# Reordering the borders and the second layer of a two-block transformer kernel on one Trainium2 core

## The reference

```
# block one, layers 1 and 2
u = rmsnorm(h, norm_pre[i]); y = mixer(u); h = h + rmsnorm(y, norm_post[i])
# dilated_mixer (layer 1): q,k,v,gate = split(u @ w_in); q,k = rope(q),rope(k)
#   windowed softmax attention of each group, groups merged by softmax of their log denominators
y = o * silu(gate) @ w_out
# diff_mixer (layer 2), per head and block of 128 queries
s = einsum(q, k) * scale                      # two score matrices, c = 0, 1
s = where(kpos <= qpos, s, -inf); p = softmax(s)
a = p[:, 0] - lam * p[:, 1]
o = rmsnorm(einsum(a, v), subln) * (1.0 - lambda_init)
y = o * silu(gate) @ w_out
# block two, twice
y = (sigmoid(gate_a) * (sparse_attention @ p_attn)
     + sigmoid(gate_b) * (gated_linear_attention @ p_gla)) @ w_out + b_out
x = layer_norm(DN_ALPHA * x + y)
u = conv3(x @ w_up) + conv_b; a, b = split(u)
x = layer_norm(DN_ALPHA * x + (gelu(a) * b) @ w_down)
```

## Time and profile before

| | |
|---|---|
| runs | 2937.83, 2944.55, 2944.97 us (median 2944.55) |
| profiled execution | 2947.25 us, span 2945.9 us, mean granted TensorE clock 0.982 |
| PE busy | 2787.2 us (95%) |
| DVE, ACT, POOL busy | 1256.2, 1092.0, 1068.4 us |
| HBM traffic | 90 GB/s over the span |

### The profile page before, as it was taken

The page is one execution under the profiler, slowest core; times in us unless marked ns, Lnnn a source line. Parts: engine busy times, 40 slices in busy tenths (PEclk is TensorE's granted clock), DMA queues, the critical chain, the costliest instruction groups (busy, mean ns, idle before and its releaser), DMA issues.

```text
span 2945.9 us, 39012 instructions
## 1 busy us (share of the span) xinstructions
PE 2787.2 (95%) x15161; PEld 2288.2 (78%) x15161; DVE 1256.2 (43%) x2777; ACT 1092.0 (37%) x2037; POOL 1068.4 (36%) x854
## 2 busy tenths in 40 slices
PE   6999999989989899999999999999999999999997
PEld 5887878788767777766688888887776668888887
DVE  3344444444455437433425424255642343542425
ACT  3444344443444433453323424233435332242422
POOL 3333334222332233332343454435342235444442
PEclk9999999999999899999999999999999999999999
DMA  4322223231111222222344232223222224423222
GB/s 143 87 87 87 82 77 94 80 125 57 60 57 56 79 92 86 72 79 82 97 150 137 72 115 77 95 86 120 72 73 78 86 86 158 134 75 100 98 89 72
DMA packets 247547, 269.06 MB, mean 91 GB/s; under 512 B 11582, under 2 KB 208930, under 8 KB 246596
## 3 DMA queue, kind: packets, MB, share of 16 engines
q1 hardware_dynamic: 247364, 266.56, 27.9%
HBM read 247.59 MB, written 18.94 MB: 90 GB/s over the span
## 4 chain that ended last, share of the span: by engine, by line
PE 80%; DVE 8%; ACT 4%; issue 3%; POOL 2%; DMA 2%; SPq 0%; DVEq 0%; ACTq 0%; POOLq 0%
PE banks L1457 43%; PE banks L1454 24%; DVE AR L2110 2%; POOL WS L2676 2%; PE banks L1475 2%; PE banks L1576 2%; PE banks L1525 1%; PE banks L1683 1%; ACT WS L1783 1%; PE banks L1559 1%; DVE SM L2110 1%; PE banks L1731 1%; PE banks L1499 1%; PE banks L1544 1%; PE banks L1647 1%
## 5 line engine op out<-in xcount | busy, mean ns | idle before, releaser
L2676 POOL TENSOR_TENSOR WS<-WR,WS 128x512 fp32r<-128x512 f32 (+1 forms) x772 | 974.1, 1294 | 1561.5 <-ACT WS L1783 1561.5
L1457 PE MATMUL banks<-WS,UT 128*128 128x512 f32 (+1 forms) x5712 | 1217.4, 363 | 26.3 <-issue 7.2
L1457 PEld LDWEIGHTS banks<-WS,UT 128*128 128x128 f32 x5712 | 920.5, 192 | 203.5 <-issue 63.4
L1454 PE MATMUL banks<-UT,WS 128*128 128x512 f32 (+1 forms) x2928 | 691.1, 395 | 0.6 <-issue 0.6
L1454 PEld LDWEIGHTS banks<-UT,WS 128*128 128x128 f32 (+1 forms) x2928 | 547.8, 189 | 128.6 <-issue 14.1
L1783 ACT ACTIVATE WS<-WR 128x1024 fp32r<-128x1024 f32 (+2 forms) x408 | 395.1, 1021 | 121.8 <-PE banks L1457 63.1
L1457 PE MATMUL banks<-WS,AT 128*128 128x256 f32 (+1 forms) x1776 | 305.6, 332 | 21.3 <-DVE AT L2110 21.3
L1457 PEld LDWEIGHTS banks<-WS,AT 128*128 128x128 f32 x1776 | 266.2, 191 | 57.6 <-DVE AT L2110 16.8
L2639 DVE SCALAR_TENSOR_TENSOR AR<-banks,AR 128x511 f32<-128x511 f32 x88 | 66.0, 750 | 227.5 <-ACT AR L2090 227.5
L2110 DVE TENSOR_TENSOR AR<-AR 128x256 f32<-128x256 f32 (+2 forms) x169 | 147.7, 893 | 18.8 <-ACT AR L2022 7.4
L2691 POOL TENSOR_TENSOR SM<-SM 128x1 f32<-128x1 f32 (+2 forms) x44 | 46.9, 1067 | 282.0 <-DVE SM L2615 121.1
(11 more groups left out here) (205 smaller groups left out, 2665.8 us busy)
## 6 DMA issues: line engine op xcount, KB each, us to landing
WR<-in_w_in SPq DMA_DIRECT2D x56, 1024.0 KB, 5.1
WR<-in_w_up SPq DMA_DIRECT2D x44, 1024.0 KB, 5.1
WR<-in_dil_w_in SPq DMA_DIRECT2D x128, 256.0 KB, 4.0
WR<-in_w_down SPq DMA_DIRECT2D x16, 1024.0 KB, 5.0
WR<-in_dil_w_in SPq DMA_DIRECT2D x8, 1024.0 KB, 5.1
WR<-in_diff_w_in SPq DMA_DIRECT2D x16, 512.0 KB, 4.3
WR<-in_diff_w_in SPq DMA_DIRECT2D x8, 1024.0 KB, 5.5
spill<-AR SPq DMA_DIRECT2D x32, 256.0 KB, 3.3
```

The source lines that it names most:

```text
L1454: mm = pe.matmul(B[bank][0:c, :], w[x][:, kk, g * P:g * P + c], act[:, y, kk, :], start=start, stop=stop)
L1457: mm = pe.matmul(B[bank][:, off:off + n], act[:, x, before_k + kk, g * P:g * P + P], w[y][:, kk, :], start=start, stop=stop)
L2676: ge.tensor_tensor(slot(i, 1)[:, s], raw(i)[:, s], slot(i, 0)[:, s].bitcast(F32), ALU.subtract).then_inc(lo_p.sem, 1)
```

## The change

It has these parts:

- **Layer 2 a step deeper.** An empty stage stands between scores and mix, and MF serves as a third score buffer. `norm2` is one step of two operations, three ticks later; the factor subln (a DMA of 128 x 1 in place of 128 x 128) is applied when the chunks of layer 2 are split.
- **No negation.** The mask step of layers 1 and 2 scales by -0.125 and takes the minimum, so the small operation behind it goes.
- **Low parts in single steps.** POOL's four quarters of a tile become four steps `lo`, one of them issued per tick, all before the tile is used.
- **Borders by parts.** Chunks 0 to 3 stand beside the gate projections; chunks 4 to 7 stand between parts of the output projection: (tile, from part, to part) = (0,0,4), (1,0,4), (0,4,6), (1,4,6), (2,0,6), (0,6,8), (1,6,8), (2,6,8). The third tile comes in at the fifth place. In `wide` with fresh input the first two token blocks go through both half tiles before the last blocks are needed.
- **The last up tile by token halves.** b10 goes as (tokens 0 to 255, both feature blocks), then (256 to 511), with its convolution, product and split by halves; d20, d21 and d22 follow with all six parts for the first block.
- **Weight tiles in halves.** Each load is two transfers with a semaphore each; half v of tile i + 2 may start when half v of tile i has been split.

```diff
+    def by_pool(self, i):
+        return i > 0 and not (self.grouped[i] and i % 2)
     def split(self):
-        self.step("split", self.splits)
+        i = self.splits
+        self.step("split", i)
+        if self.by_pool(i):
+            self.lows += [(i, v) for v in range(4)]
         self.splits += 1
+    def lower(self, i):
+        while self.lows and self.lows[0][0] <= i:
+            self.step("lo", *self.lows.pop(0))
...
     def tick(self, n=1):
...
+        for _ in range(n):
+            if self.lows:
+                self.step("lo", *self.lows.pop(0))
...
+        walk = [(half, b) for half in range(2) for b in range(first, NB)]
+        if fresh and name != "l1a0":
+            walk = [(half, b) for half in range(2) for b in (first, first + 1)]
+            walk += [(half, b) for b in range(first + 2, NB) for half in range(2)]
...
+    def opening(turns):
+        parts = [(0, 0, 4), (1, 0, 4), (0, 4, 6), (1, 4, 6), (2, 0, 6), (0, 6, 8), (1, 6, 8), (2, 6, 8)]
+        for n, what in enumerate(turns):
+            parts.insert(2 * n, what)
+        return parts
...
+                    if half and j < 2:
+                        self.soon(4, lambda: self.step("chunk", name, 2 * j))
+                        self.soon(6, lambda: self.step("chunk", name, 2 * j + 1))
...
-            yield from self.pipelined(len(units), lambda n: units[n][0] in projected, [scores, mix, turn, out_of])
+            yield from self.pipelined(len(units), lambda n: units[n][0] in projected,
+                                      [scores, lambda n: (), mix, turn, out_of])
...
+            if (kind, j) == ("b", 10):
+                i = self.open(f"f{l}b10")
+                for half in range(2):
+                    for c in range(2):
+                        self.bank[i, c, half] = 2 - 2 * half + c
+                        self.step("last", l, i, c, half)
+                        self.step("conv_last", l, i, c, half)
+                        self.tick(2)
...
-        self.by_blocks([f"f{l}d2{c}" for c in range(4)], finish, lambda: None)
+        self.by_blocks([f"f{l}d2{c}" for c in range(4)], finish, [(j, 0, 6) for j in range(3)], order=(2, 3, 0, 1))
...
-                                                    CT[:, C_CM + 512 - w:C_CM + 512], 1.0, GONE, ALU.add, ALU.max,
-                                                    SM[:, MX + 2 * e + c:MX + 2 * e + c + 1])
+                    for c in range(2):
+                        x = ve.tensor_tensor_reduce(S2(n, c, w), B[4 + c][:, 0:w], CT[:, C_CM + 512 - w:C_CM + 512],
+                                                    -0.125, -GONE, ALU.add, ALU.min, small2(n, "max", c))
                     x.then_inc(maxed.sem, 1)
-                    ve.wait_ge(maxed.sem, maxed.at["2", n])
-                    ve.tensor_scalar(SM[:, NBI + 2 * e:NBI + 2 * e + 2], SM[:, MX + 2 * e:MX + 2 * e + 2], -0.125, None,
-                                     ALU.mult).then_inc(negated.sem, 1)
...
-            def load_tile(i):
+            def load_half(i, v):
                 _, k, n, pieces = tiles[i]
                 dst = raw(i).rearrange("p (k n) -> p k n", k=k)
+                part = slice(v * k // 2, (v + 1) * k // 2)
                 for c, src in pieces:
-                    sy.dma_start(dst[:, :, c:c + src.shape[2]], src).then_inc(tile_in[i % 2].sem, 16)
+                    sy.dma_start(dst[:, part, c:c + src.shape[2]], src[:, part, :]).then_inc(tile_in[2 * (i % 2) + v].sem, 16)
```

More of the change, by code:

```diff
@@ L366, in feature_major, with by_blocks @@
             yield 2
-    def by_blocks(self, names, finish, late):
+    def by_blocks(self, names, finish, opening, order=(0, 1, 2, 3)):
         i0 = self.opened
@@ L374, in by_blocks @@
             split = b == 0
-            banks = ((0, 1, 2, 3), (4, 5), (0, 1), (2, 3))[b]
-            early = [0] * 4
-            if split:
-                for j in range(2):
-                    ws.append(self.open(names[j]))
+            banks = (order, (4, 5), (0, 1), (2, 3))[b]
+            for what in opening if split else ():
+                if isinstance(what[0], str):
+                    self.step(*what)
+                else:
+                    j, k0, k1 = what
+                    if len(ws) == j:
+                        ws.append(self.open(names[j]))
                     self.bank[ws[j], b] = (banks[j], 0)
-                    early[j] = self.tiles[ws[j]][1] - 2
-                    self.step("mm", ws[j], b, 0, early[j])
-                late()
+                    self.step("mm", ws[j], b, k0, k1)
+                    self.tick()
             for j in range(4):
@@ L525, in layer1 @@
         self.fill(self.opened + 2)
-        self.by_blocks([f"l1o{j}" for j in range(4)], self.residual("l1o"), lambda: self.last_quarter("l1g", late))
+        self.lower(self.opened + 1)
+        for x in late:
+            self.step("times", *x)
+        self.by_blocks([f"l1o{j}" for j in range(4)], self.residual("l1o"),
+                       self.opening([("chunk", "l1g", c) for c in range(4, 8)]))
     def layer2(self):
@@ L576, in layer2 @@
         self.beside(self.gates("l2g", lambda j: j in normed, late), att, R_G2)
+        self.lower(self.splits)
         self.drain(att)
+        self.flush()
         self.step("reload", "l2o")
         self.fill(self.opened + 2)
-        self.by_blocks([f"l2o{j}" for j in range(4)], self.residual("l2o"), lambda: self.last_quarter("l2g", late))
+        self.lower(self.opened + 1)
+        for x in late:
+            self.step("times", *x)
+        self.by_blocks([f"l2o{j}" for j in range(4)], self.residual("l2o"),
+                       self.opening([("chunk", "l2g", c) for c in range(4, 8)]))
     def hybrid(self, l):
@@ L760, in hybrid @@
         self.soon(1, lambda: self.step("load_gains", l))
[L761 removed]
+        self.by_blocks([f"m{l}o{j}" for j in range(4)], finish, self.opening([]))
     def ffn(self, l):
```

319 lines of the change are left out of this document (195 added, 124 removed).

## The result

| | before | changed |
|---|---|---|
| median | 2942.68 us (4 runs) | 2917.3 us (4 runs, 2912.03 to 2920.55) |
| ratio | | 0.9914, 95% interval 0.9894 to 0.9934 |
| profiled execution | 2947.25 us | 2920.55 us, span 2919.2, clock 0.987 |

A forecast was written before the change was run, and what follows sets the result against it. PE was taken as the bound, busy 2787.2 of 2945.9 us, leaving its idle and lower-clock time to win. Terms summed to 75.9 us, less 16 for new waits: 60 us net, forecast 2885 us, 8-in-10 range 2862 to 2920.

The forecast's parts named there:

- the mixers' output projections: Block two's mixer output projections: fourth tile ready some 4 us earlier through halves, 11.7 us gained, bounds 5 and 13.3.
- the last up tile: b10 by token halves: first half's convolution beside second half's products, 14.3 us gained in two layers, bounds 8 and 15.4.
- layer 2 with its border: Layer 2's attention, 17 us of 30.9 gained; its border into the output projection, 15.4 us gained.
- fresh input: Three first projections with fresh input: some waits for norms, banks or weights shortened, 8.2 us gained, bounds 3 and 13.
- layer 1's border: Layer 1 into its output projection: chunk stalls hidden beside gate products, a 3.3 us EX stall left, 9.8 us gained.
- the hybrid attention: Block two's hybrid mixers: their order stays, so no gain was forecast.
- new waits: Ten places PE reaches earlier: one more wait of 1.6 us each, -16 us, bounds 0 and 40.
- (a): Rival: ACT's queue bounds layer 2, EX the two block-one borders; 35 us gained, 2910 us; chance 0.25.
- my own sign: Layer 2's attention: the prediction is wrong if it keeps more than 20 of its 31 us.
- The third mechanism: Layer 2's attention: four `norm2` operations took 5.18 us beside POOL's low parts, then PE idled 6.08; now two operations.
- Loads in halves: Weight loads elsewhere: two half transfers cost more, hidden by 7 us of spare time; 0 us.
- The start: Kernel start: eight transfers ahead of x instead of four, -0.5 us, bounds -1.7 and +1.

The follow-up runs named there:

- e3: Changed kernel with ACT taking layer 2's exponential a stage later, in the stage the change left empty: 2894.02 us, 0.9827 of the kernel before.
- e6: Changed kernel with layer 2's empty stage taken out, so mix follows scores by one stage as before: 2917.74 us, 0.9907.
- e1: Changed kernel with open low-part steps put ahead of splitting a tile whose low part DVE makes, so loads go in tile order: 2905.13 us, 0.9863.
- e9: Changed kernel with POOL's four low-part steps right behind the split again, halves kept: 2902.22 us, 0.9862.
- e5: Changed kernel with b10 whole again, its convolution for all tokens at once, and the last down projection's opening by other parts: 2913.07 us, 0.9891.
- e7: Changed kernel with other banks for the blocks of the output and last down projections: 2909.32 us, 0.9879.
- e4: As e1, with d23, the last down projection's fourth tile, split ahead of the last step of b10's convolution: 2901.11 us, 0.9845.
- e2: As e1, with both halves of a tile loaded together once both halves of the tile two before are split: 2913.67 us, 0.9890.
- e8: Changed kernel with e1, e3, e4 (one step further), e7, earlier block-one second-tile split, layer 2's first rotations later, x fetched first: 2863.51 us, 0.9718.

## Why the prediction was wrong

Two terms failed most: the mixers' output projections (11.7 forecast, -3.6 measured) and the last up tile (14.3 forecast, about -6 measured). Both fail by the same step: the sum removes the wait that stood there and doesn't ask what is late next. By size the differences are 20 us (last up tile), 15 (mixer output projections), 12 (layer 2 with its border), 9 (fresh input) and 3 (layer 1's border), against which stand 8 us from the hybrid attention and the 16 that I had left for new waits. Of the rivals (a) is right for layer 2 (e3); its stall for EX at layer 1's border came as 1.18 us and was no bound.

- **Layer 1's border: right,** 7.1 of 9.8. The stall for EX that I left in came as 1.18, beside one of 1.83 for the second tile, whose split stands behind the last gate on ACT.
- **Layer 2's attention and border: 20.9 of 32.4.** The mechanism was named and mis-sized. I wrote that the deeper pipeline doesn't take ACT's order away, and then still took two thirds of the waits as won. In the window of the attention 17.3 us of idle time stayed, not 8, and with the clock (0.04 x 230 = 9.2) 26.5 of the 31, which by my own sign is more than 20. e6 says that the stage gave nothing, e3 that the order was worth 17. The third mechanism held: the 6.08 behind `norm2` is gone. The border had PE at the lower level for about a third of its window, as 0.83 says, not for most of it.
- **Fresh input: wrong at the first place,** -2.7 for 4.9. I moved products ahead of the turn and didn't ask what their results set off on DVE. The other two came near (0.3 for 1.1, 1.7 for 2.2), and the wait of 3.3 stood, as I had written.
- **Mixer output projections: -3.6 for 11.7, failed.** "... its load began only when all of tile two had been split. With halves the first half may be loaded 2.7 us earlier and split while the second flies". I priced the half that comes earlier and not the one that the new step order puts behind the next stage's loads (e1, e9). My sum followed the moved steps on POOL, but the loads that wait for them moved with them on SP. Some of the -3.6 is the 58.3 of one execution; the four other kernels with that order (e3, e5, e6, e7) took 53.6 to 56.9 there, which still leaves at most 2.4 us of gain. DVE and POOL slow each other besides: DVE's two low parts of w_mix_out took 2.36 us in the first mixer, with POOL at rest for most of it, and 4.12 in the second, beside POOL (rows of e1). The Trainium skill, GPSIMD Engine Reference, Specifications, has the two share their SBUF interfaces, with contention when a DVE instruction reads two inputs there, and the trace agrees. The sharpest rows for it are those of `norm2` in the kernel before (L2377): 28 of its 32 operations ran while POOL made no low part and took 0.34 to 0.35 us each, the four of the earlier trace rows ran beside POOL's low parts and took 1.34 to 1.37. The wider ones of the changed kernel take 0.68 to 0.69 us alone and 1.75 to 1.78 beside POOL, so they are slowed as well, as the prediction has it by this rule.
- **The last up tile: about -6 for 14.3, failed.** The table has -4.5, and b10's products took 11.67 us a layer, where the 48 before took 10.9. The wait of 7.90 for AT became 1.81, as predicted. What is late next wasn't asked: d23's split, behind b10's convolution on ACT, and bank 1 (e4, e5). Once both are out of the way the two stages take 39.7 and 36.1, 4.4 and 6.8 less than before; less the 1.5 of b10's products, some 10 of the 14.3 were there.
- **Loads in halves: 0, wrong by 8.** e2 shows what an early first half is worth. The 2.0 us of fixed cost that I took from the Trainium skill (DMA: Bandwidth & Descriptors, Anatomy of one DMA) stand there for transfers that GpSimd issues, and these are SP's. From the medians here, 3.6 us for 512 KB in the changed kernel and 5.1 for 1024 KB in the one before, the part that doesn't grow with the size comes to 3.6 - 1.5 = 2.1, an estimate.
- **The start: right in sum,** but PE's first turn came 2 us later, at 17.20, a little past the bound of 1.7, and fewer waits behind it gave that back.
- **The hybrid attention: 8 for 0.** That its order stays was no reason to put it at nothing: its spills go through SP's queue, and the change moved the loads in it (e9).
- **New waits: 16 us.** The allowance was of the right kind, but spread evenly over ten places. The large ones stood in five (3.60, 4.47, 6.17, 5.91 and 3.60 us) and were as large as the terms there. e8 gains 82 us; less the 12 that its start and banks bring, which my sum didn't have, that is 70, of which 6 are the hybrid attention's with its gates, against the 75.9 that I had before new waits.

## What to carry to other kernels

Where engines take their work from one list, a moved step moves everything hung on it: write out each queue, that of the loads too, and read what now stands ahead of what. For each engine that waits, ask which work behind the waiting instruction the bottleneck wants, and put that work ahead. Before the gain of a removed wait is booked, find what is late next at that place: three of the largest terms here were worth nothing until a second edit of a line or two.

## What the runs showed of the hardware

Half a tile of 512 KB landed in 3.6 us, a whole one of 1024 KB in 5.1 before. The same half at the same place was used 4.8 us after its issue in e3 and 7.5 in the changed kernel, whose orders agree there, so a border that hangs on one landing can differ by 3 us between executions. What I hadn't expected is the start: with x ahead of the weights its first transfer, issued at 0.73, was there at 5.44, where it had been used at 13.61 behind eight weight loads issued from 0.73 to 4.74, itself issued at 5.30. Of the 8.2 us won 4.6 are the earlier issue, and 3.6 the shorter time from issue to use, 4.7 in place of 8.3. That this second part is the time of the bytes ahead of it is likely, but no run shows it apart:

```profile
0.73 0.39 SPq L2852 DMA_DIRECT2D AF<-in_x  x1
...
2.11 4.56 SPq L2841 DMA_DIRECT2D WR<-in_dil_w_in  x8
5.44 1.06 ACT L1898 ACTIVATE AF<-AF 128x1024 f32<-128x1024 f32 x1 [3.43 <-DMA AF<-in_x]
```
